# A transformer layer pair on one core: zeros on TensorE at the start, the first weights' parts in pieces, the forget gates ahead of the weights

## The reference

```python
def rms_norm(x, g):
    y = xf * lax.rsqrt(jnp.mean(xf * xf, axis=-1, keepdims=True) + EPS)
    return y * g

def parallel_mixer(h, w_in, conv_w, lb, hgrn_norm, w_out):      # h = rms_norm(x, mix_norm)
    cb, cc, cx, hq, hf, hi, hg = jnp.split(h @ w_in, 7, axis=-1)
    log_f = jnp.log(lbh + (1.0 - lbh) * jax.nn.sigmoid(hf))     # forget gates
    k = (1.0 - lbh) * jax.nn.sigmoid(-hf)
    o = hgrn2_chunkwise(hq, k, hi, log_f)                       # cumulative sums of log_f, chunks of 64
    ...
```

## Time and profile before

| | |
|---|---|
| runs | 1238.59, 1241.64, 1244.49 us |
| the profiled execution | 1243.32 us, its span in the trace 1241.5 us |
| TensorE matmul busy | 1203.7 us (97%), 7842 instructions |
| VectorE busy | 900.7 us (73%) |
| ScalarE busy | 723.0 us (58%) |
| GpSimd busy | 117.9 us (9%) |
| mean granted TensorE clock | 0.990 |
| DMA | 255.43 MB, mean 206 GB/s |

### The profile page before, as it was taken

One profiled execution on the slowest core, in us unless ns is written; L12 is line 12 of the kernel. 1 busy time (PEld: TensorE's weight loads), 2 busy tenths in 40 slices (PEclk: granted clock), 3 DMA queues, 4 the chain that ended last, 5 costly groups with the idle time before them and its releaser, 6 DMA issues.

```text
span 1241.5 us, 18815 instructions
## 1 busy us (share of the span) xinstructions
PE 1203.7 (97%) x7842; PEld 1069.0 (86%) x7842; DVE 900.7 (73%) x960; ACT 723.0 (58%) x839; POOL 117.9 (9%) x137
## 2 busy tenths in 40 slices
PE   6999999999999999999999899999999999999998
PEld 6978997978888787888877788999999998989897
DVE  5897586557778878888889884758766875755554
ACT  4855224454577677776767454667778744544432
POOL 0100000000000000000000100019732520000000
PEclk8999999999999999999999999989999999999999
DMA  7433234515489888898998156533234446455552
GB/s 269 170 128 144 103 127 144 192 68 212 163 325 369 336 322 340 319 366 313 341 340 335 73 179 239 198 105 103 84 122 162 149 136 220 157 196 201 179 197 102
DMA packets 38179, 255.43 MB, mean 206 GB/s; under 512 B 4192, under 2 KB 6368, under 8 KB 10320
## 3 DMA queue, kind: packets, MB, share of 16 engines
q1 hardware_dynamic: 34800, 247.64, 55.2%
q10 hardware_dynamic: 3296, 6.61, 1.5%
HBM read 253.15 MB, written 1.08 MB: 205 GB/s over the span
## 4 chain that ended last, share of the span: by engine, by line
PE 76%; DVE 11%; ACT 7%; issue 3%; POOL 2%; DMA 1%; DVEq 0%; SPq 0%; ACTq 0%; POOLq 0%
PE bank L447 21%; PE bank L449 21%; PE bank L448 21%; DVE r L1795 4%; ACT r L1226 3%; PE bank L457 2%; PE bank L848 1%; PE bank L612 1%; PE bank L1090 1%; POOL f L2639 1%; PE bank L814 1%; PE bank L672 1%; PE bank L711 1%; DVE r L1804 1%; DMA f<-in_weights 1%
## 5 line engine op out<-in xcount | busy, mean ns | idle before, releaser
L1795 DVE TENSOR_TENSOR r<-f,r 128x2048 fp32r<-128x2048 f32 (+2 forms) x239 | 540.9, 2268 | 176.1 <-ACT r L1226 175.7
L447 PE MATMUL bank<-r,r 128*128 128x256 f32 (+5 forms) x1936 | 644.3, 333 | 12.8 <-DVE r L1795 5.8
L449 PE MATMUL bank<-r,r 128*128 128x256 f32 (+5 forms) x1936 | 633.7, 327 | 0.0
L448 PE MATMUL bank<-r,r 128*128 128x256 f32 (+5 forms) x1936 | 633.3, 327 | 0.0
L1226 ACT ACTIVATE r<-f 128x2048 fp32r<-128x2048 f32 (+3 forms) x240 | 453.3, 1891 | 171.6 <-PE bank L449 146.1
L447 PEld LDWEIGHTS bank<-r,r 128*128 128x128 f32 (+4 forms) x1936 | 359.4, 186 | 57.3 <-issue 18.1
L449 PEld LDWEIGHTS bank<-r,r 128*128 128x128 f32 (+4 forms) x1936 | 359.4, 186 | 34.6
L448 PEld LDWEIGHTS bank<-r,r 128*128 128x128 f32 (+4 forms) x1936 | 359.2, 186 | 34.5 <-issue 1.0
L1804 DVE TENSOR_TENSOR r<-f,r 128x512 fp32r<-128x512 f32 (+3 forms) x70 | 52.8, 764 | 30.5 <-ACT r L1762 11.2
L2639 POOL TENSOR_SCALAR f<-f,f 128x128 f32<-128x128 f32 (+1 forms) x64 | 63.8, 1013 | 44.6 <-DVE f L2425 44.6
L457 PE MATMUL bank<-f,f 128*128 128x128 f32 x224 | 32.1, 303 | 8.4 <-DMA f<-in_cst 6.3
(11 more groups left out here) (325 smaller groups left out, 1075.3 us busy)
## 6 DMA issues: line engine op xcount, KB each, us to landing
f<-in_weights SPq DMA_DIRECT2D x216, 1024.0 KB, 4.9
f<-in_weights SPq DMA_DIRECT2D x12, 896.0 KB, 4.7
f<-in_weights SPq DMA_DIRECT2D x8, 672.0 KB, 4.6
f<-in_weights SPq DMA_DIRECT2D x4, 882.0 KB, 5.4
f<-bias_table ACTq DMA_DIRECT2D x1, 2048.0 KB, 13.0
f<-in_mem ACTq DMA_DIRECT2D x1, 1024.0 KB, 4.7
out<-f ACTq DMA_DIRECT2D x2, 512.0 KB, 2.6
f<-in_moe ACTq DMA_DIRECT2D x1, 647.0 KB, 4.7
```

What stands on the lines that cost most here:

```text
L447: e.matmul(o, lh.r, rh.r, start=start, stop=False)
L448: e.matmul(o, lh.r, rl.r, start=False, stop=False)
L449: return e.matmul(o, ll.r, rh.r, start=False, stop=stop)
L1795: e.tensor_tensor(slot_of(n).r, slot_of(n).f, high_of(n).r.bitcast(F32), ALU.subtract).then_inc(s["w_lo"], 1)
```

## The change

It edits the program's first 45 us or so, in four places.

1. DVE writes zeros over 512 columns of a scratch tile first of all, and TensorE multiplies them three times (128x512 float32) into bank 7 ahead of its first waits for data.
2. The order of DMAs: the small first part of `sml` is issued ahead of the half of `x` on the ACT queue, the small first part of `cst` ahead of the other half on the SP queue.
3. The first weights' high part is made in two halves: the first ahead of the scaled parts' high parts, the second between the second and third of them; `high(1)`, the next unit's, stands between the third and the fourth. On DVE the first half of the low part stands behind two scaled parts instead of ahead of all, the second half ahead of the fourth scaled part.
4. The forget gates: on ACT both parts' sigmoids stand ahead of `high` of unit 3; on DVE the lower bound is applied part by part, ahead of `low` of unit 3, and the scaling of `k` behind it.

```diff
+        zeros = XNP.f[:, 512:1024]
@@ TensorE
+            e.wait_ge(s["warm"], 1)
+            for _ in range(3):
+                e.matmul(banks[7][:, :], zeros[:, 0:128], zeros, start=True, stop=True)
@@ ScalarE
-            def turn_high(q):
+            def turn_high(q, between={}):
                 for p in range(4):
                     e.wait_ge(s["n_mu"], SCALED[q] + p + 1)
                     e.activation(dst_high[pair(p)].r, dst[pair(p)].f, ACT.Copy).then_inc(s["n_hi"], 1)
+                    if p in between:
+                        between[p]()
+            e.dma_start(St[:, 0:SML_FIRST], sml[:, 0:SML_FIRST]).then_inc(s["l_s"], 16)
             e.dma_start(X[:, 0, :], x[:, 0, :]).then_inc(s["l_x0"], 16)
-            e.dma_start(St[:, 0:SML_FIRST], sml[:, 0:SML_FIRST]).then_inc(s["l_s"], 16)
...
-            high(0)
-            turn_high(0)
-            high(1)
+            def first_high(part):
+                f = slice(1024 * part, 1024 * part + 1024)
+                e.wait_ge(s[f"w{slots[0]}"], 16)
+                e.activation(high_of(0)[:, f].r, slot_of(0)[:, f].f, ACT.Copy).then_inc(s["w_hi0" if part == 0 else "w_hi"], 1)
+            first_high(0)
+            turn_high(0, {1: lambda: first_high(1), 2: lambda: high(1)})
             ahead(("hf", 0))
...
             for p in range(2):
-                if p:
-                    ahead(("hf", p))
                 wait_unit(("hf", p))
...
+            ahead(("hf", 1))
             e.wait_ge(s["hg_f"], 1)
@@ VectorE
+            e.memset(zeros, 0.0).then_inc(s["warm"], 1)
             e.wait_ge(s["l_s"], 16)
...
             diagonal(0, 1)
+            scaled(0, 0)
+            scaled(0, 1)
+            e.wait_ge(s["w_hi0"], 1)
+            first_low(0)
+            turn_low(0, 0)
+            scaled(0, 2)
+            turn_low(0, 1)
             e.wait_ge(s["w_hi"], 1)
-            first_low(0)
-            normalise(0, lambda: first_low(1))
+            first_low(1)
+            scaled(0, 3)
+            turn_low(0, 2)
+            turn_low(0, 3)
             low(1)
...
+            after(k_lb)
+            for p in range(2):
+                e.wait_ge(s["ev_a"], READ_AT["hf", p])
+                for h in (2 * p, 2 * p + 1):
+                    m = e.tensor_scalar(HF[:, h, :], HF[:, h, :], oml[:, h:h + 1], lb_[:, h:h + 1], ALU.mult, ALU.add)
+            m.then_inc(s["hg_f"], 1)
             ahead(("hf", 1))
-            e.wait_ge(s["ev_a"], READ_AT["hf", 1])
-            after(k_lb)
             for h in range(4):
-                m = e.tensor_scalar(HF[:, h, :], HF[:, h, :], oml[:, h:h + 1], lb_[:, h:h + 1], ALU.mult, ALU.add)
-                if h == 3:
-                    m.then_inc(s["hg_f"], 1)
                 m = e.tensor_scalar(KK[:, h, :], KK[:, h, :], oml[:, h:h + 1], None, ALU.mult)
@@ SyncE
+            e.dma_start(Ct[:, 0:CST_FIRST], cst[:, 0:CST_FIRST]).then_inc(s["l_c"], 16)
             e.dma_start(X[:, 1, :], x[:, 1, :]).then_inc(s["l_x1"], 16)
-            e.dma_start(Ct[:, 0:CST_FIRST], cst[:, 0:CST_FIRST]).then_inc(s["l_c"], 16)
```

More of the change, by code:

```diff
@@ L126 @@
 at_ev at_mx at_e at_rv at_sc at_ta at_y yb2_h yb2 xc_h xc cv lr_g lr_a lr_m lr_sq lr_u lr_s lr_gy gy_h gy
-gb_o ga_o mg mg_h mg2d z_r z z_h fin pad""".split()
+warm w_hi0 gb_o ga_o mg mg_h mg2d z_r z z_h fin pad""".split()
 ACT_READS = ([("hf", 0), ("hf", 1), ("hq", 0), ("hq", 1), ("hi", 0), ("hi", 1)] + [("k", j) for j in range(4)]
@@ L1836, in first_low, with normalise @@
                 m.then_inc(s["w_lo0" if part == 0 else "w_lo"], 1)
-            def normalise(q, between=None):
+            def normalise(q):
                 scaled(q, 0)
@@ L1841, in normalise @@
                 turn_low(q, 0)
-                if between is not None:
-                    between()
                 scaled(q, 2)
```

## The result

The changed kernel takes 1237.43 us (median of 7 runs) against 1242.97 us for the kernel before, run beside it; the ratio is 0.996, 95% interval 0.9944 to 0.9976. The medians lie 5.5 us apart, the interval says 3 to 7. One of the seven runs took 2410 us, for a reason that is not known, and is not in the ratio. The profiled execution took 1238.54 us, its span 1236.8 us, against 1243.32 and 1241.5: 4.7 us. The prediction was 1237.0 us and 4.6 us.

The account below looks back on a forecast made before the run. TensorE, busy 97% of the span, bounds the kernel: 2.5 us earlier plus waits of 0.6 and 1.6 gone, capped at VectorE's 4.6, so 1241.6 - 4.6 = 1237.0 us; range 1232.5 to 1241.5.

Parts of the forecast that it names:

- The zeros raise the clock: At the start: clock rises about 6.8 us, turns of x end about 10.1 instead of 12.9, worth 2.8 us there.
- The first projection: TensorE's first projection starts at 14.75 instead of 17.11 us, a gain of 2.35 us.
- the small DMAs: 28 KB and 136 KB ahead of x delay its landing by 0.4 us, to about 6.3, hidden by the zeros.
- The clock falls in the gap: TensorE idles from 11.6 to 14.75 us before the first projection; the clock was expected to fall again there.
- The first rival: Clock does not fall before the first projection; everything behind the gates 5.6 us early, 1236.0 us; chance 0.15.
- The gates: Forget gates: logarithm at 32.2 instead of 36.82 us, 4.6 us earlier; unit 4's high part at 36.2 instead of 40.84.
- The wait for unit 3: Moving low(3) back cuts its slack before TensorE needs it from 1.3 to 0.2 us; cost 0 to 0.4, taken as 0.
- The order of the parts taken alone: At the first projection: new order without the zeros' gain delays the start by 0.5 us, to 17.6.
- The second rival: Zeros don't raise the clock; logarithm 1.9 us earlier by the gates' order alone, 1.8 us gained, 1239.8 us; chance 0.13.
- The third rival: Slower: behind 130 us, four more low clock stretches cost 6.8 us, more than the 4.6 won; 1244 us; chance 0.07.
- TensorE reaches the memory's turns 2.5 us earlier: First term of the sum: first unit ends about 22.5 instead of 25.1 us, so TensorE comes 2.5 us earlier.
- a rise and a fall at other times: Clock changes elsewhere within the allowed range: TensorE alone still gains 4.0 to 5.3 us.

Follow-up runs that it names:

- the second profile: The changed kernel, same file, timed and profiled again on another chip: 1237.98 us, ratio 0.9959 to the kernel before.
- the run with zeros in the gap: Changed kernel plus six zero multiplications (256 columns each) on TensorE between second scale row and first projection: 1236.97 us, ratio 0.9951 to the kernel before.
- the best version: Changed kernel plus six zero multiplications before the first projection, gains' DMA behind x, small functions and units' parts moved: 1234.65 us, ratio 0.9933 to before.
- the one with the gates back: Changed kernel with the forget gates' old order on ScalarE and VectorE: 1239.31 us, ratio 0.9984 to the kernel before.

## Why the prediction was right

The forecast (1237.0 us, 4.6 us less) holds, and in the first profile so does each large term; in the second one a term does not (below).

- The zeros raise the clock: turns 3.81 us long, as forecast (3.7 to 4.4), and 6.41 without them. At the mark they are worth 2.0 us where the low stretches are equal. The clock rose earlier than I said, at 4.44 us, after 3.0 us of work and not 5, and the zeros ended at 5.76 and not 6.3 to 6.5. In the second profile it rose only during the turns.
- The first projection: 15.15 forecast as 14.75. The 0.4 us are x, which landed at 6.49 (6.3), and small steps of the chain to the second scale row (11.88 against 11.55). I took the small DMAs at 0.4 us by their bytes and as hidden by the zeros. Both were off. `x` landed 0.6 us later than before (6.49 against 5.89), and 0.44 of that is its later issue (1.17 instead of 0.73), which no sum by bytes holds. TensorE waited 0.84 us for it, and without the gains ahead it comes 1.1 us earlier. So `x` did come later than by the bytes; no run here separates what the two queues' turns add from what the order on one queue does.
- The clock falls in the gap all the same: 14.68, forecast 12 to 16. The first rival (it stays up) is out for this kernel, and the run with zeros in the gap shows what it would have been worth, 0.4 us against a short low stretch; I had given it 1.0.
- The gates: logarithm 31.90 (32.2), unit 4's high part 35.92 (36.2), VectorE early by 4.9 and not 4.6, the wait at the scale row gone and that for unit 7 cut from 1.6 to 0.4, where the sum left 0.1. With the gates' order back, 1.7 us of these waits return. The wait for unit 3, which I took as 0, was about 0.2 us: its first two matmuls start 0.23 and 0.19 us behind the one ahead of them (32.83, 33.06, 33.25) and not 0.113.
- The order of the parts taken alone delays the first projection: forecast 0.5, measured 0.6 from the scale row on, 0.8 with the later `x`. The second rival's sum (1.8 us in all without a rise of the clock) was too high: the run without zeros shows 1.2. It had the logarithm 1.9 us early; it was 1.1 (35.72), because ScalarE waited 1.35 us for TensorE before the second gate part.
- The third rival (more low stretches later) did not come: 17 us before, 17 us after, in the profiles. The other ten traces have between 10 and 20.5 us behind 130 us, and the best version, which starts earliest, has 20.5, as has the one with the gates back. So each 3.5 us more or less in that part moves a single time by some 1.7 us, by the estimate in the prediction; whether the time of the start has a part in it is open.

That 4.6 met 4.7 is partly luck. The first profile after had the short low stretch and the one before the long one. The term that hangs on it is the first of the sum, "TensorE reaches the memory's turns 2.5 us earlier": it was 2.6 in the first profile (38.79 against 41.41) and 0.9 in the second (40.51), where the first projection started at 15.61 and the clock rose 5.7 us behind that. The logarithm was then 3.2 us early (33.61), held by TensorE's unit 1, and the mark 3.2 us. I had allowed TensorE 4.0 to 5.3 for a rise and a fall at other times, and 3.2 lies outside. The medians say 5.5 with an interval from 3 to 7. What the length of that stretch is on average in either kernel is open: of the eight traces with the three multiplications of zeros and none in the gap it was 3.4 us in five and 6.8 in three, and these three are the ones in which the zeros took over 5.2 us; the two traces without zeros both had 6.8. Two are too few to say that the zeros shorten it.

## What to carry to other kernels

Multiplying zeros while the first rows are on their way is worth about 2 us here, because it moves the low clock out of work that others wait for; it pays only up to the moment when the rows land, and after that the zeros are the bound. What decides a gain in the first microseconds is the latest of several chains: by the marks the zeros bring 2.0 us, the gates' order 1.7 to 2.0 and the first weights' parts up to 1.35, and each does so at another wait. After that, an earlier landing of the rows, small functions that share a table, and a TensorE that stays busy through its next gap brought 3.3 us more together. Where the clock moves by itself, compare a mark in the trace between runs with the same low stretches, and profile the same kernel twice before you read a difference of a microsecond or two.

## What the runs showed of the hardware

A transfer of 28 KB in rows of 224 bytes, issued ahead of a transfer of 512 KB on the same queue, delayed that one by 1.1 us (first square of ScalarE at 6.49 against 5.39), though 28 KB at the 393 GB/s of the earlier trace rows are 0.07 us. The later issue is 0.44 us of it (1.17 against 0.73), the rest 0.66. The 136 KB in rows of 1088 bytes on the other queue did no harm to this half: with them ahead and the gains behind, `x` came at 5.28, 5.39 and 5.42 in three runs, with both behind at 5.82, 5.89 and 5.94. The Trainium skill's page on DMA (DMA: Bandwidth & Descriptors, Specifications) gives 512 bytes as the least transfer for full rate. The 0.66 us agree with it in sign, but no run changed the rows and kept the order, so they don't show that the rows are the cause.

The low stretches of one and the same kernel lay at other places and had other lengths from profile to profile (3.4 or 6.8 us at the first projection), and the first rise came once at 4.44 us and once during the turns, so that three equal multiplications took 4.31 us in one run and 5.49 in another.

The clock does not fall behind idle time alone. In the kernel before it fell at 15.53, 1.1 us after the last scale row, and at 817.7 amid 55 small matmuls (64x15) that TensorE did without a gap from 814.90 on. In the changed kernel it fell at 14.68, 2.8 us after the last scale row, and at 813.4 right behind 60 such matmuls, done without a gap from 809.81 on. With zeros in the gap it stayed up until 185 us in one kernel and until 182 in another.
